# Two transformer blocks on one core: VectorE's order of work while the first weight blocks are split

## The reference

```
h = layer_norm(concat([meta, x]), ln0_g, ln0_b)
p = h @ w_in + b_in
u_s5, q, k, v, o_pre, i_pre, f_pre, g_s5, g_m = split(p)
lam_bar = exp(lam * dt)                        # eigenvalues of the state-space mixer
b_bar = ((lam_bar - 1) / lam)[..., None] * b_mat
state = scan(lam_bar, b_bar @ u);  y = Re(c_mat @ state) + d * u
...                                            # mLSTM, mixing, feed-forward
```

## Time and profile before

| | |
|---|---|
| median of 3 runs | 889.69 us (883.49 to 891.09) |
| profiled execution, its own time | 887.35 us |
| its span | 885.6 us |
| PE busy | 806.3 us, 91% |
| DVE busy | 580.8 us, 66% |
| ACT busy | 462.7 us, 52% |
| POOL busy | 227.2 us, 26% |
| mean granted TensorE clock | 0.956 of full |

### The profile page before, as it was taken

One profiled execution on the slowest core, in us unless ns is written; L12 is line 12 of the kernel. 1 busy time (PEld: TensorE's weight loads), 2 busy tenths in 40 slices (PEclk: granted clock), 3 DMA queues, 4 the chain that ended last, 5 costly groups with the idle time before them and its releaser, 6 DMA issues.

```text
span 885.6 us, 16172 instructions
## 1 busy us (share of the span) xinstructions
PE 806.3 (91%) x6157; PEld 767.8 (87%) x6157; DVE 580.8 (66%) x814; ACT 462.7 (52%) x734; POOL 227.2 (26%) x187
## 2 busy tenths in 40 slices
PE   4799999998899869999999966998696999999998
PEld 3699999987899859998999965977595989999997
DVE  7966678743776556676665658884446778666673
ACT  5775664466564334454445333556653645555553
POOL 5000000001023032254232213643352313334320
PEclk9999999999899969999999995999996999999998
DMA  6363433153455627778686830624142466555531
GB/s 232 101 187 124 139 101 115 48 170 97 139 167 188 242 83 254 253 255 298 238 310 230 293 112 1 238 86 174 35 145 86 147 238 215 186 189 174 189 110 48
DMA packets 45719, 146.96 MB, mean 166 GB/s; under 512 B 9293, under 2 KB 10061, under 8 KB 45665
## 3 DMA queue, kind: packets, MB, share of 16 engines
q1 hardware_dynamic: 44544, 144.88, 48.5%
q10 hardware_dynamic: 1120, 1.34, 0.5%
HBM read 144.07 MB, written 1.05 MB: 164 GB/s over the span
## 4 chain that ended last, share of the span: by engine, by line
PE 62%; issue 13%; DVE 12%; POOL 7%; ACT 4%; DMA 2%; POOLq 0%; DVEq 0%; SPq 0%; ACTq 0%
PE ps L473 20%; PE ps L688 18%; PE ps L701 9%; POOL gl L2026 3%; POOL relu L2023 2%; PE ps L909 2%; PE ps L673 2%; DMA raw<-in_w_stream 1%; DVE tg_m L1751 1%; DVE wl L1422 1%; PE ps L519 1%; DVE ada_acc L1769 1%; PE ps L533 1%; DVE small L1747 1%; PE ps L548 1%
## 5 line engine op out<-in xcount | busy, mean ns | idle before, releaser
L1422 DVE TENSOR_TENSOR wl<-raw,wh 128x1024 fp32r<-128x1024 f32 x200 | 250.3, 1253 | 156.8 <-ACT wh L971 155.6
L971 ACT ACTIVATE wh<-raw 128x1024 fp32r<-128x1024 f32 x220 | 231.1, 1053 | 114.2 <-DMA raw<-in_w_stream 61.1
L688 PE MATMUL ps<-xh,wh 128*128 128x256 f32 x720 | 211.6, 294 | 23.1 <-POOL xl L2014 23.1
L688 PE MATMUL ps<-xl,wh 128*128 128x256 f32 x720 | 207.9, 289 | 0.0
L688 PE MATMUL ps<-xh,wl 128*128 128x256 f32 x720 | 207.6, 288 | 0.0
L688 PEld LDWEIGHTS ps<-xh,wh 128*128 128x128 f32 x720 | 141.6, 197 | 28.7 <-issue 18.1
L688 PEld LDWEIGHTS ps<-xh,wl 128*128 128x128 f32 x720 | 141.9, 197 | 0.0
L688 PEld LDWEIGHTS ps<-xl,wh 128*128 128x128 f32 x720 | 141.6, 197 | 0.2
L473 PE MATMUL ps<-xh,wh 128*128 128x256 f32 (+1 forms) x416 | 123.1, 296 | 6.4 <-DVE wl L1422 5.4
L701 PE MATMUL ps<-gh,wh 128*128 128x256 f32 x432 | 122.6, 284 | 4.5 <-POOL gl L2026 2.6
L701 PE MATMUL ps<-gh,wl 128*128 128x256 f32 x432 | 121.9, 282 | 0.0
(11 more groups left out here) (369 smaller groups left out, 1309.0 us busy)
## 6 DMA issues: line engine op xcount, KB each, us to landing
raw<-in_w_stream SPq DMA_DIRECT2D x220, 512.0 KB, 3.9
ada_w<-in_w_ada SPq DMA_DIRECT2D x48, 512.0 KB, 4.3
vtk<-in_x SPq DMA_DIRECT2D x2, 512.0 KB, 4.7
out<-ob SPq DMA_DIRECT2D x4, 256.0 KB, 2.0
u<-uT SPq DMA_DIRECT2D x16, 34.0 KB, 2.5
eepp<-in_s_mats SPq DMA_DIRECT2D x1, 512.0 KB
bti<-btr SPq DMA_DIRECT2D x16, 32.0 KB, 2.6
ws<-in_w_s ACTq DMA_DIRECT2D x1, 512.0 KB, 3.9
```

Of the source, the lines that this page charges most:

```text
L688: mm = nc.tensor.matmul(ps[:, bank, 0:SEQ], w, x, start=(k == 0), stop=(k == 3 * KD - 1))
L971: nc.scalar.activation(wh[:, b % RING], raw[:, b % RING], ACT.Identity).then_inc(hi_done, 1)
L1422: V.tensor_tensor(wl[:, b % RING], raw[:, b % RING], wh[:, b % RING].bitcast(F32), ALU.subtract).then_inc(lo_dve, 1)
```

## The change

VectorE makes the low part of block 3 (the fourth) directly behind that of block 2, ahead of `eigenvalues()`; that of block 4 directly behind `eigenvalues()`; then `angles(1)` and the low part of block 5. Products 0, sums 0 and products 1 then follow one another with no low part between them, and from `lo(6)` on the order is the old one. The set of instructions is the same, and no other engine's program is edited.

```diff
             angles(0)
             lo(2)
+            lo(3)
             eigenvalues()
+            lo(4)
+            angles(1)
+            lo(5)
...
             for b in range(B_U, B_GLU):
-                if b == 0:
-                    angles(1)
                 if 1 <= b < 17:
                     (power_products if b % 2 else power_sums)((b - 1) // 2)
...
-                lo(b + AHEAD)
+                if b >= 3:
+                    lo(b + AHEAD)
             head_stat(HEADS - 1)
```

## The result

The changed kernel takes 881.28 us (median of 20 runs, 876.05 to 886.23); the kernel before 891.22 us in the same comparison. The medians lie 9.9 us apart; the ratio follows the means instead (881.6 and 890.3, without one run of the kernel before that took 2688 us). It is 0.9902, with a 95% interval of 0.9878 to 0.9925, so about 8.7 us less, just inside the 1% for which I had given 0.71. The forecast was 882.3 us, in a range of 876.5 to 889.0. The profiled execution took 881.33 us with a span of 879.5, 6.1 us under that of before.

A forecast was written before the change was run, and what follows sets the result against it. TensorE bounds the kernel, idling 4.26 us ahead of a slow block 3. 4.43 + 1.64 = 6.07 us off 887.35 gives 881.3; one microsecond added for the median makes 882.3 us, range 876.5 to 889.0.

The forecast's parts named there:

- the sum of 6.07: Pause of 4.43 us plus clock gain of 1.64 us, all ahead of block 4, nothing given back behind it.
- Term one: Ahead of block 3: low part 3 moved up lets block 3 follow block 2 without a pause, 4.43 us.
- Term two: Block 3 keeps full clock and takes block 2's length, 3.09 instead of 4.73 us: 1.64 us, bounds 0 and 1.64.
- Costs taken as nothing: Later eigenvalues, low parts 4 and 5, angles(1), high part 7 and load 10 were to delay no block.
- VectorE's room at block 6: Low part 6 stays at its old time while block 6 moves up; slack shrinks from 7.7 to 1.6 us.
- The catching up at low part 12: VectorE, without its earlier idles, was to wait for ScalarE's high part 12 again, by 2.5 us.
- The rival with late loads: VectorE at block 6 or load 10 becomes the bound; gain 3 us or nothing, 886 or 888 us; chance 0.08.
- The sign that I named: Behind 100 us: a mean clock differing from before would show the prediction wrong.

The follow-up runs named there:

- The middle position: Kernel before with low part 3 put between the eigenvalue chain and angles(1); ratio 0.9926 (0.9899 to 0.9954).
- the repeats: Changed kernel with products 1 computed once, twice or three times more behind themselves; TensorE's wait ahead of block 6: none, 1.02 and 2.34 us.
- three repeats: Changed kernel with products 1 computed three more times, VectorE 4.0 us late; block 2 to the copy behind block 9 took 35.15 us against 31.06.
- one and two repeats: Changed kernel with products 1 computed once or twice more, VectorE 1.3 or 2.6 us late; no wait and a 1.02 us wait ahead of block 6.
- the pooled runs: Unchanged kernels over the first three comparisons: 81 runs of the kernel before, mean 889.4 us; 30 of the changed kernel, mean 881.9 us.
- the filled kernel: Kernel before with 32 extra matmuls between blocks 2 and 3, low part 3 left late; ratio 0.9943 (0.9909 to 0.9977).

## Why the prediction was right

The mechanism came as forecast: both terms and the places that were to cost nothing are in the trace. That the median lies only 1 us from the forecast of 882.3 is in part luck. The forecast started at 888.35 us (887.35 and a microsecond), the runs of the kernel before in the comparison had a mean of 890.3, and the measured gain was 2.7 us more than the sum of 6.07; the two differences nearly cancel.

**Term one, the pause.** Forecast 4.43 us. Block 3 started 35.63 - 28.11 = 7.52 us after block 2 before, and 31.11 - 28.02 = 3.09 after: 4.43. The middle position isolates it in part: 2.5 us earlier gave a pause 2.5 us shorter.

**Term two, the clock.** Forecast 1.64, the upper bound. Block 3 took 34.29 - 31.11 = 3.18 us instead of 4.73, so 1.55; with term one that makes the 5.98. Filling the pause alone gave 1.47. The Trainium skill's remark that the number of slow matmuls at a start varies between runs (page TensorE: Matmul & The Clock Gate, section "What's actually happening") hardly showed here: block 3 took 4.73 and 4.78 us in two executions. It showed later in the run: in the 6 us behind one and the same pause of 2.60 us, 30 matmuls ran at a mean clock of 0.72 in the changed kernel, and 21 at 0.50 with low part 3 alone moved.

**Costs taken as nothing.** Low part 4 and low part 5 were in time. ScalarE waited 0.38 us for angles(1), where I had 0.3, and high part 7 began at 39.55 (forecast 40.0), covered as said. High part 10 began at 48.63, straight behind a copy and with no wait for its load, and block 10 started 65.63 - 28.11 = 37.52 us after block 2 before and 31.55 after: 5.97 of the 5.98 are still there. The experiment with low part 3 alone shows what moving low parts 4 and 5 as well was worth, 0.17 us.

**VectorE's room at block 6.** Forecast 1.6 us; measured between 1.3 and 2.6 by the repeats, and 1.0 us of wait for 2.6 of lateness. The catching up at low part 12 came as forecast, 2.64 us of wait for 2.5.

**What was mis-sized.** The rival with late loads gives 886 us for a gain of 3, but 887.35 - 3 is 884.4. In the same rival, "the gain is lost on the way", I took lateness at its length. The run with three repeats shows that a late low part of that kind costs up to 1.8 us more, through the clock.

**What lies behind block 6** is where the prediction said least. It let everything there simply move up by 6.1 us. These are the same five pauses, first before, then after (block 3's is in the earlier trace rows; the first two of before stand in the earlier trace rows):

```profile
543.20 0.55 PE L688 MATMUL ps<-xh,wh 128*128 128x256 f32 x1 [5.19 <-POOL xl L2014]
...
578.00 0.97 PE L763 MATMUL ps<-qs,cst 128*128 128x256 f32 x2 [1.28 <-ACT qstd L1255]
...
873.47 5.46 PE L951 MATMUL ps<-cst,sq 128*128 128x1 f32 x32 [1.02 <-ACT sq L1401]
```

```profile
211.65 0.67 PE L605 MATMUL ps<-vtk,eepp 16*128 16x257 f32 x2 [2.60 <-ACT hraw L1100]
...
226.57 0.69 PE L638 MATMUL ps<-cst,hraw 128*128 128x128 f32 x2 [3.05 <-DVE hraw L1705]
...
536.10 0.55 PE L688 MATMUL ps<-xh,wh 128*128 128x256 f32 x1 [5.20 <-POOL xl L2017]
...
574.25 0.67 PE L763 MATMUL ps<-qs,cst 128*128 128x256 f32 x2 [1.28 <-ACT qstd L1255]
...
868.35 4.44 PE L951 MATMUL ps<-cst,sq 128*128 128x1 f32 x32 [1.03 <-ACT sq L1401]
```

The lead is 6.12 us at the first, 4.49 at the second, 7.10 at the third, 3.75 at the fourth, 5.12 at the last, and 6.1 at the end. The second profiles of both kernels give 5.95, 4.41, 7.03, 3.67, then 1.87 at the last and 0.0 at the end. So the lead isn't carried through unchanged. Up to the fourth pause the two pairs agree to 0.2 us; behind it they part by 6 us, and the 6.1 at the end of the first pair is no proof that the lead came through. For the whole kernel only the many runs speak.

The sign that I named, another mean clock behind 100 us, did not come: it is 0.96 from 100 to 870 us in all four profiles. But the clock fell in other places. Between the first and the second pause it fell after a 2.60 us pause that had left it alone in both profiles of before. At the fourth, 1.28 us long, it fell in both profiles of before and in neither of the changed kernel (length, busy times, clock as above; before, then after):

```profile
578.00:582.00 4.00, 4.00 (x17) 3.66 (x18) 3.89 (x9) 2.03 (x3) 0.00 (x0) 0.57 0.38 131
```

```profile
574.25:578.25 4.00, 4.00 (x30) 3.90 (x31) 3.90 (x9) 2.02 (x3) 0.00 (x0) 1.00 0.38 131
```

Between the third and the fourth TensorE waits for VectorE, 0.7 to 1.1 us each time, in the second block's q and k, which neither profile of before has (total, count and longest, in us):

```profile
PE ps L798 <- DVE qrot L1828: 1.1, 1, 1.1
```

There a VectorE multiplication takes 1.88 us instead of 0.71. Each is shown with the low part that GpSimd makes meanwhile (first before, then after):

```profile
563.18 0.71 DVE L1831 TENSOR_TENSOR kf<-kf,qstd 128x256 f32<-128x256 f32 x1
560.98 2.63 POOL L1983 TENSOR_TENSOR wl<-raw,wh 128x1024 fp32r<-128x1024 f32 x1 [0.36 <-ACT wh L971]
```

```profile
558.21 1.88 DVE L1834 TENSOR_TENSOR kf<-kf,qstd 128x256 f32<-128x256 f32 x1
557.42 2.38 POOL L1986 TENSOR_TENSOR wl<-raw,wh 128x1024 fp32r<-128x1024 f32 x1 [1.31 <-ACT wh L971]
```

GpSimd is at work in both kernels, and in both the multiplication ends 0.28 to 0.29 us after GpSimd does (563.89 and 563.61; 560.09 and 559.80). So it is held until GpSimd's instruction is through, and its length tells only how early in that instruction it began. Two more of VectorE's instructions there read the same way in each kernel (2.59 and 1.58 us after; 0.68 and 0.66 before). Free of GpSimd the same multiplication takes 0.42 us (at 579.75 before). The reciprocals among them, 1.75 us each, are not held.

These waits stand in both profiles of the changed kernel and in four of its relatives (low part 3 alone, in the middle, one and two repeats), and in none of before, the filled pause, the three repeats, the version with low part 2 moved too and the two with later pauses filled. What puts VectorE and GpSimd into the one phase or the other was not tried and stays open. So does the share of the 1 to 2.6 us by which the first comparison and the pooled runs show more than 6.1.

## What to carry to other kernels

Look for the instruction that the matrix engine waits for and ask what stands ahead of it in its own engine's queue that nobody needs yet: one move of 1.2 us of work gave 5.8 of the 6.0 us. Price a pause of TensorE as its length and, where the clock falls behind it, the slow block too: 1.5 to 1.8 us more here behind pauses of 2.34 and 4.26 us, at most 0.25 behind those of 1.02 and 1.74. Where a pause can't be removed, fill it. After such a move, compute the new slack of the next blocks from the old trace; it held to 0.1 us here, while everything hundreds of microseconds later has to be taken with a scatter as large as the gain, so take more than one profile of each kernel before reading anything there.

## What the runs showed of the hardware

- **The clock and pauses.** In the stretch with 24 matmuls to a block, the clock held after pauses of 0.7, 1.02, 1.36 and 1.74 us and fell after 1.93 (inside block 0, where low part 2 was moved too), 2.34 and 4.26. Later in the run length alone doesn't order the cases. Behind the 3.05 us pause it was down in every profile that has it. At 2.6 us, always the same pause ahead of the last numerators, it did either: no fall in both profiles of before and with three repeats, a fall in the eight others that have it. At 1.28 us, above, it did either too. In the filled kernel and with three repeats the 2.60 us pause ended at nearly the same time (216.08 and 216.14), and only in the first did the clock fall, so time since the start doesn't decide it (the matmul behind the pause, then the 4 us from there, columns as above):

```profile
216.08 0.67 PE L610 MATMUL ps<-vtk,eepp 16*128 16x257 f32 x2 [2.60 <-ACT hraw L1105]
216.08:220.08 4.00, 4.00 (x15) 3.34 (x16) 1.39 (x2) 2.50 (x4) 0.46 (x1) 0.61 0.18 45
```

```profile
216.14 0.67 PE L605 MATMUL ps<-vtk,eepp 16*128 16x257 f32 x2 [2.60 <-ACT hraw L1100]
216.14:220.14 4.00, 4.00 (x27) 3.56 (x28) 2.09 (x2) 2.50 (x4) 0.47 (x1) 1.00 0.19 57
```

- **Two vector engines at once.** In the cases read here a subtraction, addition or multiplication of two tensors that starts while the other engine makes one is held until that one is through. VectorE's reciprocals and its multiplication that reads PSUM (0.42 us at 560.07 before, beside a GpSimd low part) are not. GpSimd's subtraction of 128 x 272 took 3.13 us instead of 0.76 and ended 0.7 us after two VectorE subtractions of 128 x 1024 in a row. In the other direction VectorE's low part 1 takes 1.74 us instead of 1.23 in both kernels, where it meets the last of GpSimd's, and its multiplications of 128 x 256 end 0.28 to 0.29 us after the low part that GpSimd was making. VectorE work put closer together can so delay GpSimd work that nothing in the program ties to it.
